# A feed-forward layer's up products in pairs as Strassen products, with the down halves dealt among them

## The reference

```python
h2 = rms_norm(x, norm2_w)
x = x + jnp.square(jax.nn.relu(h2 @ w_ff_in)) @ w_ff_out
```

## Time and profile before

| what | us |
|---|---|
| median of 3 runs (1585.23 to 1585.51) | 1585.36 |
| the profiled execution | 1585.56 |
| its span, first to last instruction | 1583.4 |
| of it the first feed-forward part (504.5 to 852.9) | 348.4 |
| PE, DVE, ACT, POOL busy in the span | 1566.8, 720.7, 683.7, 799.8 |
| granted TensorE clock (1 is 2.4 GHz) | 0.998 |

### The profile page before, as it was taken

One profiled execution on the slowest core, in us unless ns is written; L12 is line 12 of the kernel. 1 busy time (PEld: TensorE's weight loads), 2 busy tenths in 40 slices (PEclk: granted clock), 3 DMA queues, 4 the chain that ended last, 5 costly groups with the idle time before them and its releaser, 6 DMA issues. The chain is left out here.

```text
span 1583.4 us, 22348 instructions
## 1 busy us (share of the span) xinstructions
PE 1566.8 (99%) x7546; PEld 1260.4 (80%) x7546; DVE 720.7 (46%) x1363; ACT 683.7 (43%) x1108; POOL 799.8 (51%) x1060
## 2 busy tenths in 40 slices
PE   9999999999999999999999999999999999999998
PEld 6687777777888888888887887778988888888886
DVE  5496986664233212121123446663334651552354
ACT  6435786554334423232233434553643442342333
POOL 6444654233455554545455542256545655555553
PEclk9999999999999999999999999999999999999999
DMA  5322222213232232323232421133323233233231
GB/s 191 103 94 68 82 90 69 66 54 120 94 100 99 93 102 91 100 93 106 92 107 94 127 86 51 45 119 111 117 86 101 80 106 107 80 106 105 81 104 70
DMA packets 46132, 149.91 MB, mean 95 GB/s; under 512 B 4648, under 2 KB 9904, under 8 KB 46064
## 3 DMA queue, kind: packets, MB, share of 16 engines
q1 hardware_dynamic: 39648, 140.00, 27.5%
q10 hardware_dynamic: 6416, 8.98, 1.7%
HBM read 146.73 MB, written 2.11 MB: 94 GB/s over the span
## 5 line engine op out<-in xcount | busy, mean ns | idle before, releaser
L312 POOL TENSOR_TENSOR w_lo<-w_raw,w_hi 128x256 fp32r<-128x256 f32 x1056 | 799.6, 791 | 761.3 <-ACT w_hi L1012 760.8
L1012 ACT ACTIVATE w_hi<-w_raw 128x1024 fp32r<-128x1024 f32 x264 | 274.8, 1051 | 297.9 <-PE job L346 286.4
L344 PE MATMUL job<-a_hi,w_hi 128*128 128x512 f32 (+1 forms) x986 | 382.2, 388 | 1.7 <-POOL w_lo L312 1.0
L346 PE MATMUL job<-a_hi,w_lo 128*128 128x512 f32 (+1 forms) x986 | 377.1, 382 | 0.0
L345 PE MATMUL job<-a_lo,w_hi 128*128 128x512 f32 (+1 forms) x986 | 377.0, 382 | 0.0
L344 PE MATMUL job<-b_hi,w_hi 128*128 128x512 f32 x936 | 369.5, 395 | 0.9 <-DVE sq L1591 0.5
L346 PE MATMUL job<-b_hi,w_lo 128*128 128x512 f32 x936 | 364.6, 389 | 0.0
L345 PE MATMUL job<-b_lo,w_hi 128*128 128x512 f32 x936 | 364.3, 389 | 0.0
L344 PEld LDWEIGHTS job<-a_hi,w_hi 128*128 128x128 f32 x986 | 185.3, 188 | 56.2 <-issue 12.3
L346 PEld LDWEIGHTS job<-a_hi,w_lo 128*128 128x128 f32 x986 | 185.3, 188 | 36.5
L345 PEld LDWEIGHTS job<-a_lo,w_hi 128*128 128x128 f32 x986 | 185.4, 188 | 34.5
(11 more groups left out here) (345 smaller groups left out, 1482.4 us busy)
## 6 DMA issues: line engine op xcount, KB each, us to landing
w_raw<-w_all SPq DMA_DIRECT2D x264, 512.0 KB, 3.4
arena<-x_t ACTq DMA_DIRECT2D x8, 512.0 KB, 5.6
out_t<-arena SPq DMA_DIRECT2D x6, 256.0 KB, 2.1
arena<-rg_w ACTq DMA_DIRECT2D x1, 1024.0 KB, 6.3
arena<-mem_t ACTq DMA_DIRECT2D x1, 1024.0 KB, 6.6
spare<-row_table ACTq DMA_DIRECT2D x3, 256.0 KB, 4.4
arena<-consts ACTq DMA_DIRECT2D x1, 512.0 KB, 4.1
out_t<-arena ACTq DMA_DIRECT2D x2, 256.0 KB, 2.1
```

What stands on the lines that cost most here:

```text
L312: nc.gpsimd.tensor_tensor(w_lo[:, sl, c], raw[:, sl, c], w_hi[:, sl, c].bitcast(F32), ALU.subtract).then_inc(s("lo_ready"), 1)
L344: mm(ps[:, 0:n], w_hi[:, sl, c], hi[:, kt, 0:n], start=kt == 0, stop=False)
L346: ins = mm(ps[:, 0:n], w_lo[:, sl, c], hi[:, kt, 0:n], start=False, stop=kt == last)
L1012: fn(w_hi[:, sl], raw[:, sl], ACT.Copy).then_inc(s("hi_ready"), 1)
```

## The change

The 32 up jobs become 4 plain ones and 14 **pairs**. A pair is the product of a 2 x 2 arrangement: two output tiles by two halves of the inner dimension for the weights (W11, W12, W21, W22, each 128 x 512), and two halves of the inner dimension by two halves of the tokens (256 each) for the input. Instead of 8 such products it makes 7 (Strassen's, in the form with few sums): of W11, W21, W22, of the sums T1 to T4 of the weights, and of x and four sums of its parts. Each product is 4 blocks x 3 matmuls of 256 columns.

- POOL makes T1 to T4 (`ff_sum`) and the low parts of W11, W21, W22, of the plain jobs and of the last eight down halves, now in instructions of 512 columns.
- ACT makes all high parts in instructions of 512 columns (`ff_high`), 11 a pair. It copies three PSUM quarters a pair to SBUF (`copy_u1`, `copy_u2`, `copy_p5`), since products are accumulated on them later.
- DVE makes the low parts of T1 to T4 and of the down halves (`sum_low`), adds three sums (`c11`, `c22`, `c12`), activates, and makes the hidden low parts from squares that ACT now writes to a PSUM bank (`square_ps`). rstd also lies in a PSUM bank. Before the pairs it makes the sums of x (`half_sums`) and their low parts (`half_rests`).
- Down jobs are cut into halves by the inner dimension, of 4 blocks each; four stand among the products of a pair, and eight at the end. A half is added to x on its own.
- The slots of weights are halved to eight places; `ff_units` lists the order in which units take them, with one place left empty in odd pairs. ACT may fill a place when PE has used what lay in it.
- The loops are written out for this part.

```diff
+def ff_units():
+    order = [("job", f, half) for f in range(4) for half in range(2)]
+    for n in FF_BLOCKS:
+        d = ff_downs(n)
+        order += [("W11", n), ("W21", n), d[0], ("T2", n), ("T1", n), d[1]]
+        if n % 2 == 1 and n < FF_PAIRS - 1:
+            order.append(None)
+        order += [("T3", n), ("W22", n), d[2]] if n < FF_PAIRS - 1 else [("T3", n), d[2], ("W22", n)]
+        order += [("T4", n), d[3]]
+    return order + [("D", 7, d) for d in range(8)]
...
 SP
+                elif f % 4 == 0:
+                    sp.wait_ge(s("ff_sum"), FF_SUM["T4", n])
+                elif f % 4 == 1:
+                    sp.wait_ge(s("ff_raw_low"), FF_RAW["W22", n])
+                else:
+                    sp.wait_ge(s("ff_sum_low"), FF_SUMMED[ff_downs(n)[2 * (f % 4) - 3]])
...
 POOL
+            for n in FF_BLOCKS:
...
+                ff_sum("T1", n, ff_block("W12", n), ff_block("W11", n))
+                ff_sum("T2", n, ff_block("W22", n), ff_source(("T1", n)))
+                ff_low("W11", n)
+                ff_low("W21", n)
+                ff_sum("T3", n, ff_block("W22", n), ff_block("W12", n))
+                ff_sum("T4", n, ff_block("W21", n), ff_source(("T2", n)))
+                ff_low("W22", n)
...
 PE
+            def ff_p1(n):
+                if n > 2:
+                    pe.wait_ge(s("ff_part"), FF_PART["act", n - 1, 0])
+                ff_product("W11", n, ff_c1, x_part(0, 0), True)
...
+            for n in FF_BLOCKS:
+                d = ff_downs(n)
+                ff_p1(n)
+                ff_p2(n)
+                down(d[0])
+                ff_p6(n)
+                ff_p5(n)
+                down(d[1])
+                ff_p7(n)
+                if n < FF_PAIRS - 1:
+                    ff_p3(n)
+                    down(d[2])
...
+                ff_p4(n)
+                down(d[3])
...
 ACT
+            def ff_high(*tag):
+                u = FF_UNIT[tag]
...
+                before = [FF_ORDER[i] for i in range(u - 2 * SLOTS, -1, -2 * SLOTS) if FF_ORDER[i]]
+                if before:
+                    act.wait_ge(s("ff_used"), FF_USED[before[0]])
...
+                copy_u1(n)
+                if n < FF_PAIRS - 1:
+                    e = ff_downs(nxt)
+                    ff_high(*d[2])
+                    ff_high("T4", n)
+                    ff_high(*d[3])
+                    copy_u2(n)
+                    ff_high("W11", nxt)
+                    copy_p5(n)
+                    ff_high("W21", nxt)
+                    ff_high(*e[0])
+                    ff_high("T2", nxt)
+                    square(n, 1)
+                    ff_high("T1", nxt)
+                    ff_high(*e[1])
+                    square(n, 0)
+                    ff_high("T3", nxt)
+                    ff_high("W22", nxt) if nxt < FF_PAIRS - 1 else ff_high(*e[2])
...
 DVE
+                if n > 2:
+                    down_add(ff_downs(n - 1)[3])
+                    hidden_low(n - 1, 0)
+                sum_low(*d[2])
+                c11(n)
+                sum_low("T4", n)
+                down_add(d[0])
+                sum_low(*d[3])
+                activate_c11(n)
+                down_add(d[1])
+                if n < FF_PAIRS - 1:
+                    e = ff_downs(nxt)
+                    sum_low(*e[0])
+                    c22(n)
+                    sum_low("T2", nxt)
+                    c12(n)
+                    activate_second(n)
+                    sum_low("T1", nxt)
+                    down_add(d[2])
+                    hidden_low(n, 1)
+                    sum_low(*e[1])
+                    activate_c21(n)
+                    sum_low("T3", nxt)
...
             for f in range(8):
-                add_to_x(J_FF + 56 + f, f)
+                down_add(("D", 7, f))
+                dve.wait_ge(s("ff_added"), 56 + f + 1)
                 prep(2, f, "mix", b_hi, b_lo)
```

More of the change, by code:

```diff
@@ L307, in _, with ff_sum @@
+            def ff_sum(w, n, a, b):
+                if n >= 4:
+                    pool.wait_ge(s("ff_sum_low"), FF_SUMMED[w, n - 2])
+                if w in ("T2", "T4"):
+                    pool.wait_ge(s("ff_sum"), FF_SUM[w, n] - 1 if w == "T2" else FF_SUM["T2", n])
+                nc.gpsimd.tensor_tensor(ff_source((w, n)), a, b, ALU.subtract).then_inc(s("ff_sum"), 1)
+            with pool.Fori(0, J_IN2 // SLOTS) as i:
                 for sl in range(SLOTS):
                     pool.wait_ge(s("hi_ready"), i * SLOTS + (sl + 1))
[L310 to L313, removed]
+                    low(sl)
@@ new lines, in plain, with ff_product @@
+            def plain(f, half, kts):
+                return ff_half(("job", f, half), kts, plain_ps[f], b_hi, b_lo, 0, 7)
+            def ff_product(w, n, ps, xs, first):
+                ff_wait((w, n))
+                wh, wl = ff_tile(w_hi, (w, n)), ff_tile(w_lo, (w, n))
+                for kt in range(4):
+                    c, (xh, xl) = slice(kt * P, kt * P + P), xs(kt)
+                    mm(ps, wh[:, c], xh, start=first and kt == 0, stop=False, skip_group_check=True)
+                    mm(ps, wh[:, c], xl, start=False, stop=False, skip_group_check=True)
+                    ins = mm(ps, wl[:, c], xh, start=False, stop=kt == 3, skip_group_check=True)
+                ins.then_inc(s("ff_used"), 1)
@@ L622, in in2_jobs @@
+            down(("D", 7, 0), 0)
+            down(("D", 7, 1), 0)
+            down(("D", 7, 0), 1)
+            down(("D", 7, 1), 1)
+            for d in range(2, 8):
+                down(("D", 7, d))
             def in2_jobs(first, n):
@@ L1298, in _ @@
-            with act.Fori(0, 2) as i:
-                for c in range(4):
-                    split(J_FF + 3 + c, i + 12)
-                    ff_hidden(c, 3, i)
+            ff_high("job", 3, 0)
+            ff_high("job", 3, 1)
+            norm_root_all(2)
+            ff_high("W11", 2)
+            s_high(2)
+            ff_high("W21", 2)
+            s_high(3)
+            ff_high("D", 0, 0)
+            act.wait_ge(s("norm_inv"), 2)
+            fn(t_ps[0][:], rstd[:], ACT.Copy).then_inc(s("ff_copied"), 1)
```

504 lines of the change are left out of this document (398 added, 106 removed).

## The result

The change makes the kernel slower, by a little: 1587.72 us, median of 20 runs (1586.90 to 1589.66), where the kernel before takes 1585.55 us in 20 runs beside it. The ratio is 1.0014, 95% interval 1.0008 to 1.0020. Forecast was 1579.7, with 1588.0 as the upper end: the time is inside the range, but on the wrong side of no change.

What follows compares the result with a forecast made beforehand. PE, busy 99% of the span, was taken to bound the kernel, so only its own stream pays. The terms -11.2 + 5.2 + 0.3 = -5.7 us from 1585.36 gave 1579.7 us, range 1574.0 to 1588.0.

Steps and rivals of the forecast that it cites:

- The gain of PE's own stream: First feed-forward part: a pair takes 10.08 us instead of 10.88, over 14 pairs 11.2 us less.
- POOL's 512 columns at 1.33: POOL's 512-column instructions in the pair blocks: 1.33 us each, 9.3 us a block; 1.40 at the other end.
- Turn by turn, whole instructions: Where DVE and POOL meet: they alternate by whole instructions; a DVE low part of weights can wait up to 1.3 us.
- rival D: Pair blocks: POOL with its next instruction queued keeps the port; 28 us back, 1602 us; chance 0.13 with milder forms.
- The steady stall: Chain from P3 to the next P1: 0.78 us late after odd blocks, 0.07 after even ones, 5.2 us back.
- the right base: Whole kernel: the forecast starts from the runs' median, 1585.36 us.
- What else is moved: Its first line, the start: half sums and rests of x between the preps; hidden, nothing, or 1 us once if exposed.
- have four banks and wait for nobody: First two hidden pairs, at the start of the part: no wait, no cost.
- The end: Last eight down halves: some 2.1 us of DVE backlog, slack 1.7; between 0 and 0.8 us, taken as 0.3.
- rival C: Pair blocks: stalls eat the gain, POOL at 1.43 or chain 0.4 longer everywhere; 1582.2 to 1588.5 us, chance 0.20.
- The signs named as "wrong": PE idle absent, before every pair, before P6, P7, P3, P4, or beyond 0.8 us at the end; DVE instructions of 2 us.

Runs made afterwards that it cites:

- e10_rests_late: Bank-scaled kernel with T2 and end reorders: low parts of half sums 2, 3 between first activations, hidden tile 3's ahead of T3's; 1576.14 us.
- e3_no_half_sums: Changed kernel with zeros written in place of the half sums of x, their five instructions a tile left out; 1579.76 us.
- e8_scaled_in_bank: Changed kernel with DVE still making the scaled tile of x, but in a free PSUM bank; 1581.24 us.
- e1_t2_behind: Changed kernel with DVE making c12 and the second activation before T2's low part in every block; 1584.83 us.
- e4_end_order: Changed kernel with the down sum ahead of the previous tile's low part in the last eight down halves; 1586.42 us.
- e6_first_pair: Kernel of three edits (ACT-scaled tiles): first pair's hidden tile 3 squared ahead of two weight copies, its low part ahead of T3's; 1579.14 us.
- e2_scaled_on_act: Changed kernel with ACT making the scaled tile of x, to SBUF and to a PSUM bank, instead of DVE; 1582.00 us.
- e7_more_switches: Kernel of three edits (ACT-scaled tiles) with a block's first three down halves cut in two, a product between the pieces; 1586.03 us.

## Why the prediction was wrong

**What held.** The gain of PE's own stream: 0.1200 a matmul, 10.08 a pair, 11.2 in all, confirmed by the closed ledger of e10_rests_late. POOL's 512 columns at 1.33: the mean of the 58 low parts is 1.34 recorded, and 1.28 to 1.30 where DVE is quiet; the sums T1 to T4, which meet DVE's low parts more often, take 1.54 and 1.58 on the mean (L460, 52 of them between 528 and 855 us). Turn by turn, whole instructions: rival D, in which POOL keeps the port, does not happen; the longest low part of weights takes 1.61 us. The steady stall, by place and by cause: c12 of an odd block was forecast 15.71 us after the block's start and came at 572.22 - 556.52 = 15.70. That the even pairs wait and the odd ones don't is as told. And the time was computed from the right base.

**The step that failed** is the first line of "What else is moved": "hidden, nothing; if it were exposed, 1 us once". It is 4.6 us, and 3.8 more in the first pair, for which "have four banks and wait for nobody" was all that was said. Two errors are in it. The working took 3.8 us for a tile's sums and low part as if DVE were alone, though it had shown before that DVE and POOL take turns and had a price for a meeting in the earlier trace rows; what stands between the adds was forecast to delay job 6 by 0.9, and delayed it by 4.6 (its add stands at 499.37 in the trace of before, not at 499.6 as the prediction read). And free banks are no cover: the first pair waits for the hidden tiles themselves, through a chain on ACT and DVE that starts only behind all half sums, the reciprocal and the low parts; that chain was never written down with times. e3_no_half_sums shows the size of both (8.0 us), e8_scaled_in_bank the cause of the most (6.5), e10_rests_late the last of it (1.0, with the swap that it holds as well).

**Terms that were mis-sized.** The steady stalls: 2.8 instead of 5.2. c12 was on time; from there the chain took 577.91 - 572.22 = 5.69 us instead of 5.88, and P1 itself was due 0.12 later, since the block takes 21.08 and not 20.96. In even blocks c12 came 14.70 after the start instead of 14.96. The end: 1.15 instead of 0.3, above the bound of 0.8. The six rounds from 837.60 to 855.36 take 17.76, which is 6 x 2.72 and 1.44 of the delays that the prediction counted (the product with the constants, two splits; the third comes too late to matter). What it missed is in the order of the work: the first two halves of the eight are dealt in pieces, half 0 ends at 837.17 and half 1 only 1.36 later (last starts of their matmuls), so PE makes halves 0 to 6 in 14.96, not in 16.32. The backlog is 2.8, and a slack of about 1.7 leaves 1.1. The change of shape, 1.6, was not in the list.

**The rivals.** The time lies in rival C's interval, but C's mechanism (stalls in every block) did not happen; it was right by the number alone. The signs named as "wrong" did their work: the idle beyond 0.8 at the end did occur. None was named for the stretch before the first block, and that is where the trace had to be read first.

**The clock.** In the changed kernel's trace PE idles from 509.8 to 512.1, and from 513.4 to 516.8 the granted clock is 0.50, that is 1.2 GHz; this makes 1.7 of the 4.6 us. In the kernels without that idle the clock stays at 1.00 there. The wait of 2.0 us before 535 is followed by the same fall in e1_t2_behind and in e4_end_order, but not in the changed kernel. In e1_t2_behind:

```profile
531.80:536.20 4.40, 2.56 (x21) 2.32 (x20) 3.09 (x5) 2.88 (x6) 0.00 (x0) 1.00 0.00 0
536.20:539.60 3.40, 3.40 (x13) 2.92 (x12) 3.01 (x5) 2.48 (x6) 1.35 (x1) 0.50 0.00 0
```

This second fall costs nothing: the slower matmuls fill the time in which PE otherwise waits at 540.24, that wait is gone in both traces, and the first pair's block takes 24.75 and 24.70 us, against 24.75 in the changed kernel. So half clock costs only where no wait behind it takes the loss in. The clock also falls where PE had been at work, near the end of e6_first_pair:

```profile
1560.90:1564.30 3.40, 3.13 (x26) 2.84 (x25) 1.16 (x3) 2.53 (x4) 0.00 (x0) 1.00 0.01 2
1564.30:1567.70 3.40, 3.40 (x17) 3.40 (x18) 0.68 (x3) 0.26 (x1) 0.00 (x0) 0.50 0.02 5
```

The traces of e2_scaled_on_act and e7_more_switches have such a fall as well (from 1569.2 and 1572.6), and these three take 730.8 to 731.4 us behind the part, where those of the other kernels with pairs take 729.3 to 729.5. It also bears on times without a trace: three of the eleven runs of e7_more_switches took 1587.06 to 1587.17 at a mean granted clock of 0.997, the other eight 1585.48 to 1586.25 at 0.998. So differences of about 1 us between two medians are safe only where the part in the trace shows them too.

## What to carry to other kernels

Cost what a change moves in front of its loop by the same rules as the loop itself: the one-off work ahead of the first block and in the first pair lost 8.4 us of an 11.2 us gain, the stalls in the loop that got all the care 2.8. Where DVE and GpSimd work at the same time, count which DVE instructions have all operands in SBUF, and put an intermediate tile in a free PSUM bank, if the bank's own price (here 0.75 for 0.49 us) is less than the wait; on a queue, let what frees a bank or feeds PE go ahead of what is not yet due. Before moving an instruction, see whether its engine idles there: here a gain came from filling a wait, and the edit that only changed the order of work around it made the part 0.9 us longer.

## What the runs showed of the hardware

A TENSOR_SCALAR of 512 columns with SBUF at both ends waits for GpSimd (1.51 us beside it, 0.49 where it is quiet), and into PSUM it does not (0.75). A DVE subtraction of 1024 columns takes 2.32 beside GpSimd's 512-column ones and 1.22 alone. Matmuls of 512 columns behind ones of 256 step by some 0.003 to 0.010 us more than 0.2267 for most of the first nine matmuls, 0.03 us in all; those of 256 behind 512 don't differ from 0.120.
